# One score step per decay level of the gated linear attention, instead of two

## The reference

```
def step(s, inp):
    ...
    b = jnp.cumsum(ac.astype(jnp.float32), axis=2)
    rel = b[:, :, :, None, :] - b[:, :, None, :, :]
    decay = jnp.where(lower_tri, jnp.exp(jnp.minimum(rel, 0.0)), 0.0)
    scores = jnp.einsum('bhid,bhjd,bhijd->bhij', qf, kf, decay)
    o = (jnp.einsum('bhcd,bhde->bhce', qf * jnp.exp(b), s)
         + jnp.einsum('bhij,bhje->bhie', scores, vf))
```

## Time and profile before

| | |
|---|---|
| median of 3 runs | 3193.57 us (3192.23 to 3196.89) |
| the profiled execution, its own time | 3192.06 us |
| its span in the profile | 3190.3 us |
| PE busy | 3071.9 us, 96% of the span |
| DVE busy | 1802.5 us, 57% |
| ACT busy | 1483.3 us, 46% |
| the chain that ended last | PE 83%, DVE 9%, ACT 3%, issue 3%, DMA 2% |
| DMA | mean 174 GB/s |

### The profile page before, as it was taken

One profiled execution on the slowest core, in us unless ns is written; L12 is line 12 of the kernel. 1 busy time (PEld: TensorE's weight loads), 2 busy tenths in 40 slices (PEclk: granted clock), 3 DMA queues, 4 the chain that ended last, 5 costly groups with the idle time before them and its releaser, 6 DMA issues.

```text
span 3190.3 us, 54273 instructions
## 1 busy us (share of the span) xinstructions
PE 3071.9 (96%) x23160; PEld 2791.2 (87%) x23160; DVE 1802.5 (57%) x2837; ACT 1483.3 (46%) x2222; POOL 151.5 (5%) x147
## 2 busy tenths in 40 slices
PE   7999999999999999999999989999999999999998
PEld 5899888898779998899898879999899999989997
DVE  4445554655456545455555555465766656576665
ACT  3344444453544443344443444456654444665443
POOL 0000000001000000000200000001010101101000
PEclk9999999999999999999999999999999999999999
DMA  7765444654445555765355345554355654434553
GB/s 272 281 211 170 149 157 167 211 196 145 140 150 184 180 181 195 264 214 166 128 176 173 106 159 198 184 174 133 113 164 184 200 192 150 138 104 160 180 198 132
DMA packets 409691, 556.67 MB, mean 174 GB/s; under 512 B 25276, under 2 KB 357996, under 8 KB 409068
## 3 DMA queue, kind: packets, MB, share of 16 engines
q1 hardware_dynamic: 409452, 553.20, 52.0%
HBM read 552.12 MB, written 1.05 MB: 173 GB/s over the span
## 4 chain that ended last, share of the span: by engine, by line
PE 83%; DVE 9%; ACT 3%; issue 3%; DMA 2%; SPq 0%; POOL 0%; DVEq 0%; ACTq 0%
PE psum L118 24%; PE psum L120 23%; PE psum L119 23%; DVE wl L275 1%; PE psum L709 1%; DVE wl L2172 1%; DMA wr<-in_ffn_w_dram 1%; PE psum L2337 1%; PE psum L2421 1%; PE psum L1527 1%; PE psum L2443 1%; PE psum L126 1%; PE psum L1182 1%; PE psum L1883 1%; PE psum L1898 1%
## 5 line engine op out<-in xcount | busy, mean ns | idle before, releaser
L275 DVE TENSOR_TENSOR wl<-wr,wh 128x1024 fp32r<-128x1024 f32 (+1 forms) x558 | 658.0, 1214 | 221.3 <-ACT wh L264 220.2
L264 ACT ACTIVATE wh<-wr 128x1024 fp32r<-128x1024 f32 (+1 forms) x558 | 555.0, 1039 | 249.3 <-DMA wr<-in_ffn_w_dram 218.9
L118 PE MATMUL psum<-xt_hi,wh 128*128 128x256 f32 (+1 forms) x2000 | 570.2, 285 | 4.7 <-DVE wl L275 3.6
L119 PE MATMUL psum<-xt_lo,wh 128*128 128x256 f32 (+1 forms) x2000 | 560.8, 280 | 0.0
L120 PE MATMUL psum<-xt_hi,wl 128*128 128x256 f32 (+1 forms) x2000 | 560.6, 280 | 0.0
L2172 DVE TENSOR_TENSOR wl<-wr,wh 128x1024 fp32r<-128x1024 f32 (+3 forms) x336 | 392.0, 1202 | 121.8 <-ACT wh L2164 120.4
L118 PEld LDWEIGHTS psum<-xt_hi,wh 128*128 128x128 f32 (+1 forms) x2000 | 377.0, 188 | 17.8 <-issue 10.4
L119 PEld LDWEIGHTS psum<-xt_lo,wh 128*128 128x128 f32 (+1 forms) x2000 | 376.1, 188 | 2.2
L120 PEld LDWEIGHTS psum<-xt_hi,wl 128*128 128x128 f32 (+1 forms) x2000 | 377.2, 189 | 0.1
L118 PE MATMUL psum<-wh,xt_hi 128*128 128x256 f32 (+1 forms) x1280 | 369.8, 289 | 2.8 <-ACT vv L3322 1.8
L2164 ACT ACTIVATE wh<-wr 128x1024 fp32r<-128x1024 f32 (+3 forms) x336 | 322.7, 997 | 99.9 <-DMA wr<-in_mlp_w_dram 72.7
(11 more groups left out here) (490 smaller groups left out, 5455.6 us busy)
## 6 DMA issues: line engine op xcount, KB each, us to landing
wr<-in_ffn_w_dram SPq DMA_DIRECT2D x231, 1024.0 KB, 5.2
wr<-in_w_in_dram SPq DMA_DIRECT2D x88, 1024.0 KB, 5.1
wr<-in_w_mod_dram SPq DMA_DIRECT2D x72, 1024.0 KB, 4.9
wr<-in_mlp_w_dram SPq DMA_DIRECT2D x64, 1024.0 KB, 5.3
wr<-in_w_out_dram SPq DMA_DIRECT2D x20, 1024.0 KB, 5.5
wr<-in_mem_w_kv_dram SPq DMA_DIRECT2D x8, 1024.0 KB, 5.2
wr<-in_w_branch_dram SPq DMA_DIRECT2D x16, 512.0 KB, 3.4
wr<-in_w_branch_dram SPq DMA_DIRECT2D x8, 1024.0 KB, 5.3
```

The source lines that it names most:

```text
L118: pe.matmul(out, a[0], b[0], start=first, stop=False)
L119: pe.matmul(out, a[0], b[1], start=False, stop=False)
L264: act.activation(self.high[s][:, r], self.raw[s][:, r], ACT.Copy).then_inc(self.highs.sem, 1)
L275: dve.tensor_tensor(self.low[s][:, r], self.raw[s][:, r], self.high[s][:, r].bitcast(F32), ALU.subtract).then_inc(self.lows.sem, 1)
```

## The change

The two score steps of a level become one, for all four heads. It runs the same eight matmuls in two halves of four. The heads of a half are now h and h+2 (in banks 4 and 5), and PE waits between the halves on a semaphore of its own, `level_half`, that the last matmul of the first half raises. One DVE instruction then takes 128x1024 out of both banks. The step count of the stage falls from 26 to 17, and from 27 to 18 with the start. The cover table's step numbers of the three level stages are rewritten with the same counts (4 and 4; 2, 4 and 5; 10 and 3), and the cover of two matmuls ahead of `xm.out` is dropped. The covers of the attention stages keep their step numbers.

```
-        self.order = [("decay", 0, 0), ("score", -1, 0), ("score", -1, 1)]
+        self.order = [("decay", 0), ("score", -1)]
         for m in range(n):
-            self.order += [("decay", m + 1, 0)] if m + 1 < n else []
-            self.order += [("score", m, 0), ("score", m, 1)]
+            self.order += [("decay", m + 1)] if m + 1 < n else []
+            self.order.append(("score", m))
...
-                for t in range(2):
-                    jt, it = (t, 1 - t) if m == GLA_LEVELS else (t, t)
-                    for i in range(2):
-                        r = slice(32 * (2 * pair + i), 32 * (2 * pair + i) + 32)
...
+                for half in range(2):
+                    if half == 1:
+                        last.then_inc(self.sc_half.sem, 1)
+                        pe.wait_ge(self.sc_half.sem, self.sc_half.at(m + 2))
+                    for t in range(2):
+                        jt, it = (t, 1 - t) if m == GLA_LEVELS else (t, t)
+                        for i in range(2):
+                            r = slice(32 * (2 * i + half), 32 * (2 * i + half) + 32)
...
-                u = self.unit(m, pair)
-                dve.wait_ge(self.sc_ready.sem, self.sc_ready.at(u + 1))
-                if u >= 2:
-                    dve.wait_ge(self.sc_taken.sem, self.sc_taken.at(u - 1))
-                src = self.w.ps[:, 4:6, pair * 256:(pair + 1) * 256]
-                hs = slice(2 * pair, 2 * pair + 2)
+                dve.wait_ge(self.sc_ready.sem, self.sc_ready.at(m + 2))
+                if m >= 0:
+                    dve.wait_ge(self.sc_taken.sem, self.sc_taken.at(m + 1))
+                src = self.w.ps[:, 4:6, :].rearrange("p a (b t n) -> p (a b t) n", b=2, t=2)
...
-                    last = dve.copy_predicated(near[:, hs, :, :].rearrange("p h t n -> p (h t) n"),
-                                               self.lev[:, m, :].unsqueeze(1).to_broadcast([P, 4, P]),
-                                               src.rearrange("p h (t n) -> p h t n", t=2))
+                    last = dve.copy_predicated(near[:, :, :, :].rearrange("p h t n -> p (h t) n"),
+                                               self.lev[:, m, :].unsqueeze(1).to_broadcast([P, 2 * GLA_HEADS, P]), src)
...
-    zm.levels.cover, xm.levels.cover, xm1.levels.cover = {0: 5, 4: 4, 23: 4}, {0: 2, 2: 4, 17: 5}, {0: 10, 5: 3}
-    zm.na_turn.cover, xm.out.cover = {0: 7}, {0: 2}
+    zm.levels.cover, xm.levels.cover, xm1.levels.cover = {0: 5, 3: 4, 15: 4}, {0: 2, 1: 4, 11: 5}, {0: 10, 3: 3}
+    zm.na_turn.cover = {0: 7}
```

More of the change, by code:

```diff
@@ L1484, in __init__ @@
         n = self.n = GLA_LEVELS + 1
-        self.order = [("decay", 0, 0), ("score", -1, 0), ("score", -1, 1)]
+        self.order = [("decay", 0), ("score", -1)]
         for m in range(n):
-            self.order += [("decay", m + 1, 0)] if m + 1 < n else []
-            self.order += [("score", m, 0), ("score", m, 1)]
+            self.order += [("decay", m + 1)] if m + 1 < n else []
+            self.order.append(("score", m))
         if exi is not None:
-            self.order.append(("start", 0, 0))
+            self.order.append(("start", 0))
         self.n_steps = len(self.order)
@@ L1506, in pe @@
         self.ready(pe)
-        for kind, m, pair in self.order:
+        for kind, m in self.order:
             if kind == "decay":
@@ L1521, in pe @@
                 w.open(pe, 5)
-                for t in range(2):
-                    jt, it = (t, 1 - t) if m == GLA_LEVELS else (t, t)
-                    for i in range(2):
-                        r = slice(32 * (2 * pair + i), 32 * (2 * pair + i) + 32)
-                        src = self.qk[r, :] if m < 0 else self.dq[r, m % 2, :]
-                        last = pe.matmul(w.ps[:, 4 + i, pair * 256 + t * P:pair * 256 + (t + 1) * P], src[:, 256 + jt * P:256 + (jt + 1) * P],
-                                         src[:, it * P:(it + 1) * P], start=True, stop=True)
+                for half in range(2):
[6 more added lines that the diff above has]
+                            r = slice(32 * (2 * i + half), 32 * (2 * i + half) + 32)
+                            src = self.qk[r, :] if m < 0 else self.dq[r, m % 2, :]
+                            last = pe.matmul(w.ps[:, 4 + i, half * 256 + t * P:half * 256 + (t + 1) * P], src[:, 256 + jt * P:256 + (jt + 1) * P],
+                                             src[:, it * P:(it + 1) * P], start=True, stop=True)
                 last.then_inc(self.sc_ready.sem, 1)
                 for bank in (4, 5):
-                    w.hold(bank, lambda pe_, n=self.unit(m, pair) + 1: pe_.wait_ge(self.sc_taken.sem, self.sc_taken.at(n)))
+                    w.hold(bank, lambda pe_, n=m + 2: pe_.wait_ge(self.sc_taken.sem, self.sc_taken.at(n)))
             else:
@@ L1558, in dve @@
                 if m >= 2:
[L1559 removed]
+                    dve.wait_ge(self.sc_ready.sem, self.sc_ready.at(m))
                 s = 2 ** m
```

11 lines of the change are left out of this document (5 added, 6 removed).

## The result

The changed kernel takes 3212.97 us (median of 14 runs), the kernel before 3193.64 us beside it: ratio 1.006, 95% interval 1.0045 to 1.0075. It is 19 us slower. The forecast was +5.2 us with a range up to 3209, so it missed in size. The profiled execution takes 3210.04 us, its span is 3208.2 us.

What follows compares the result with a forecast made beforehand. PE, busy for 96% of the span, was taken as the bound. Terms A to E, 2.2 - 7.1 + 8.6 - 0.5 + 2.0 = +5.2 us, took 3193.57 to 3198.8 us; range 3187 to 3209 for 8 in 10.

Steps and rivals of the forecast that it cites:

- Term A: PE's own time in the 27 merged score steps: 1.74 us each for 1.66, together +2.2 us.
- r: Restart time between the first half's end and the second half in a merged step: taken as 0.20 us.
- rival 2: Faster, chance 0.20: restart costs PE only 0.05, old waits go, new ones are largely given back; -6.6 us, 3187.0 us.
- Term B: PE's waits of score and decay steps for `near` all go: -7.1 us.
- Term C: New PE waits at adjacent steps, start of `xm1`, end of `xm` and `GlaState` of `zm`: +8.6 us, bounds 2.9 and 12.
- D: Covers: two dropped ahead of `xm.out`, those of the levels keep their number; -0.5 us.
- Term E: Background behind the levels comes nine steps earlier, so attention products wait for the way over ACT: +2.0 us (0 to 4).
- Rival 1: Slower, chance 0.37: three more clock falls behind waits of 1.2 us or more, 4.9 us; +10.1 in all, 3203.7 us.
- its three windows: 355 to 440, 725 to 800 and 1554 to 1620 us: two clock falls forecast there, five would be rival 1.
- the forecast case: The main sum, +5.2 us to 3198.8 us, chance 0.43; said to span 3194 to 3200 us.
- the clock rival: Rival 1 by another name; its upper end, 3209 us, was the top of the forecast range.

Runs made afterwards that it cites:

- e1: Changed kernel with an empty background step behind each score step and the covers of the kernel before: 3182.6 us, ratio 0.9964 to the kernel before.
- e2: Changed kernel with nine empty background steps behind each level stage: 3193.9 us, ratio 0.9998 to the kernel before.
- e18: Changed kernel itself, unedited, measured and profiled again: 3210.1 us, ratio 1.0051 to the kernel before.
- e7: Changed kernel with nine empty steps just ahead of the attention stages of the first block's z and x mixers: 3206.0 us, ratio 1.0045 to the kernel before.
- e11: Kernel of e7 with the 18 small bias-table loads spread over six foreground pieces: 3201.4 us, ratio 1.0021 to the kernel before.
- e5: Changed kernel with covers moved to where its trace shows PE waiting, in levels, end state and attention: 3195.2 us, ratio 1.0009 to the kernel before.
- e9: Kernel before, two narrow score steps kept, with covers added at five waits for `near`: 3195.2 us, ratio 0.9998 to the kernel before.
- e12: Kernel of e1 without the covers inside the level stages of the x mixers: 3179.7 us, ratio 0.9933 to the kernel before.
- e6: Kernel of e1 with a second wait of PE for itself in the second half of each merged step: 3189.4 us, ratio 0.9988 to the kernel before.

## Why the prediction was wrong

**Term A, the wrong sign.** r was taken as 0.20, from waits of PE for another engine, and is 0.07. By the forecast's own sum a merged step costs 1.54 + 0.07 = 1.61 where two narrow ones cost 1.66, so A is -1.4 us and not +2.2. The forecast had named the sign of it, a row under 1.5 us; it is 1.49. The page Advanced Engine Details and Errata of the Trainium skill (Miscellaneous Facts, Network/Comms) has 50 to 100 ns for reading a semaphore. The measured stillness of 0.07 us agrees with it, so the estimate that the forecast set beside its own was the better one, and rival 2 was right on this term.

**Term B, half right.** The waits for `near` went (0.3 us left in e1), but most of the 7.1 came back as other waits, and PE's stillness fell by 2.2. What made up for it I had left out: the clock falls behind those waits go too (390.8 and 414.7 us in the earlier trace rows). e1, which is A and B alone, gains 10.8 where A + B said 4.9.

**Term C, the waits right.** Three adjacent waits of 1.49 (I had 1.63), 1.0 at the start of `xm1` (1.2), 0.7 at `far` (1.0). With D this part was + 6.6, and e1 to e2 measures + 11.3: stillness + 5.2, and 20 us at 1.2 GHz instead of 10. `kd` was mis-sized, 3.6 for a share of 1.5, since I followed the chain and not DVE's list, in which a weight split stands ahead of `kd`. It lies behind the levels, so its wait comes between e2 and the changed kernel.

**Term E, the step that failed.** "Nine steps fewer shift everything behind ... I take +2.0 us (0 to 4)." The step from e2 to the changed kernel is 19 us (17 with e18), which holds E and the wait for `kd`, together 3.5 in the forecast. I counted only the products that had lost a cover, and took 1.75 us, the way over an idle ACT, as the longest wait. The runs show three things in its place: copies that come to stand behind a split, a table load and a `silu` in ACT's list; the burst of loads on SP, which the thinner background uncovers (e7, e11); and the clock falls behind each of these waits. In the three stretches PE's stillness grows by 8.4 us (8.6 in e18), its busy time by 13.4 (7.6). The bounds of E were bounds of a case in which ACT is free; I took ACT's low share of the earlier trace rows for room.

**Rival 1 had the mechanism and not the place.** It said that more waits of 1.2 us and above would pull the clock down, with three more falls at 1.6 each. In its three windows the profile shows five falls, at 355, 372, 400, 427 and 727 us, the number I had named for it. That hit is partly luck: the falls at 355 and 727 have their like in the kernel before, at 353 and 718, beginning just outside the windows, so like for like it is one more than before. Four more lie in the attention (451, 509, 837, 861 us), where it did not look. In z and x the changed kernel's falls cost 11 to 14 us more than those before in the first profile and 3 to 5 in the second (by the busy times, and by half of the time at 1.2 GHz). A wait does not always bring one: that of 1.49 us at 759 us was followed by none, and the same wait in e18 by one. The page TensorE: Matmul & The Clock Gate (Part 1) of the Trainium skill has it that activity releases the throttle. e5, where products on the identity hold 0.99 to 1.00 while the dependencies stay, agrees; the 41 us at 1.2 GHz do not, since in e9 PE stands for less than 0.15 us at a time in them.

**Sum.** The chain of kernels measures -10.8 (A, B), +11.3 (C without `kd`, D), +19 (E, `kd`). These add to the 19 us by construction, as each is the distance to the next kernel. My net for the same parts was -4.9 + 6.6 + 3.5: each sign right, and the last part short by 15.6, which is more than the whole miss of 14 us. Two bounds were worked out wrongly as well: with the bounds of A and E together the forecast case spans 3192.7 to 3202.4 us and not 3194 to 3200, and the clock rival with the upper bound of A and half of the rise of C ends at 3207, not 3209. Neither would have held the 3213.

## What to carry to other kernels

Before a background stage is shortened, list what stands behind it on every in-order engine and on the DMA queue at its new place; on a kernel whose covers fit one order, the shift can cost more than the edit gains, and empty steps in the old places (e1, e12) keep the gain. Before an idle time is charged to PE, see whether it is PE's or its weight load's. Where PE is 96% busy, price a wait by what the clock does behind it too. Compare kernels by stretches cut at the same foreground instruction, since a median can hang on an event elsewhere.

## What the runs showed of the hardware

- When PE waits for its own last matmul, PE stands for 0.07 us and the load of the next weights for 0.26 (6.9 us in 27 times, 14.0 in 54). The second wait in a step of e6 makes the step 0.34 us longer (1.83 for 1.49).
- A copy over two PSUM banks in one DVE instruction runs at about the rate of one bank: 128x1024 in 1.22 us, 1.33 when masked, against 0.69 and 0.74 for half.
- The 41 us at 1.2 GHz near 1815 us lengthen the stretch from matmul 10000 to 11200 from 241.9 us (before) to 260.5 (e9). They come in 11 of 20 profiled executions. None of e12's eight times, the highest 3182.1 us, stands apart as if it had them. The cause stays open.
